# One 512-column product of the rounded weights over the high and low parts, in all stages with 256 columns

## The reference

```
h = h + mix @ w_out                                   # first block
g = silu(conv(x @ w_gate)); h = h + (g * (x @ w_up)) @ w_down
proj = rms_norm(h) @ w_in_2                           # second block
m = sig(g0)*(ya @ w_br_a) + sig(g1)*(yb @ w_br_b) + sig(g2)*(yc @ w_br_c)
h = h + m @ w_out_2
h = h + (silu(x @ w_gate_2) * (x @ w_up_2)) @ w_down_2
out = rms_norm(h)
```

## Time and profile before

| | |
|---|---|
| median of 3 runs | 2632.57 us |
| profiled execution, its own time | 2633.74 us |
| its span | 2632.1 us |
| TensorE busy | 2608.5 us (99%), 22866 products |
| VectorE busy | 1658.2 us (63%) |
| ScalarE busy | 1252.0 us (48%) |
| mean DMA rate | 189 GB/s |

### The profile page before, as it was taken

One profiled execution on the slowest core, in us unless ns is written; L12 is line 12 of the kernel. 1 busy time (PEld: TensorE's weight loads), 2 busy tenths in 40 slices (PEclk: granted clock), 3 DMA queues, 4 the chain that ended last, 5 costly groups with the idle time before them and its releaser, 6 DMA issues.

```text
span 2632.1 us, 58075 instructions
## 1 busy us (share of the span) xinstructions
PE 2608.5 (99%) x22866; PEld 2578.4 (98%) x22866; DVE 1658.2 (63%) x2223; ACT 1252.0 (48%) x1563; POOL 85.8 (3%) x123
## 2 busy tenths in 40 slices
PE   9999999999999999999999999999999999999998
PEld 8999999999999999999999999999999999999998
DVE  7778786666666555555556776656665555655554
ACT  6456654434444444434445564444554444444443
POOL 0000000000000000000111500000000000000000
PEclk9999999999999999999999999999999999999999
DMA  7543446555565566666555455556555555566655
GB/s 251 156 140 120 150 168 200 192 199 199 183 209 185 205 190 207 199 193 193 190 191 174 160 183 195 200 196 199 194 198 194 197 194 191 191 193 207 199 192 185
DMA packets 138876, 497.83 MB, mean 189 GB/s; under 512 B 16544, under 2 KB 17056, under 8 KB 138752
## 3 DMA queue, kind: packets, MB, share of 16 engines
q1 hardware_dynamic: 135728, 491.34, 56.0%
q0 software_dynamic: 3024, 4.66, 0.9%
HBM read 493.31 MB, written 2.62 MB: 188 GB/s over the span
## 4 chain that ended last, share of the span: by engine, by line
PE 92%; DVE 4%; ACT 2%; DMA 1%; issue 1%; DVEq 1%; SPq 0%; ACTq 0%
PE acc L1372 30%; PE acc L1373 29%; PE acc L1374 29%; DVE wlo L841 1%; PE aux L1425 1%; DMA h<-in_hT 1%; ACT whi L480 1%; PE aux L1405 0%; PE aux L1503 0%; DMA raw<-in_wts 0%; DVEq L914 0%; PE aux L1416 0%; PE aux L1506 0%; PE aux L1619 0%; DVE qn_na L987 0%
## 5 line engine op out<-in xcount | busy, mean ns | idle before, releaser
L841 DVE TENSOR_TENSOR wlo<-raw,whi 128x1024 fp32r<-128x1024 f32 x926 | 1120.6, 1228 | 706.7 <-ACT whi L480 703.2
L1372 PE MATMUL acc<-xh,whi 128*128 128x256 f32 (+3 forms) x4968 | 1377.2, 277 | 4.3 <-DVE wlo L841 2.0
L1374 PE MATMUL acc<-xh,wlo 128*128 128x256 f32 (+3 forms) x4968 | 1367.4, 275 | 0.0
L1373 PE MATMUL acc<-xl,whi 128*128 128x256 f32 (+3 forms) x4968 | 1367.4, 275 | 0.0
L480 ACT ACTIVATE whi<-raw 128x1024 fp32r<-128x1024 f32 x926 | 958.9, 1054 | 791.6 <-PE acc L1374 774.3
L1372 PEld LDWEIGHTS acc<-xh,whi 128*128 128x128 f32 (+1 forms) x4968 | 951.0, 191 | 11.0 <-issue 5.9
L1373 PEld LDWEIGHTS acc<-xl,whi 128*128 128x128 f32 (+1 forms) x4968 | 951.2, 191 | 0.4
L1374 PEld LDWEIGHTS acc<-xh,wlo 128*128 128x128 f32 (+1 forms) x4968 | 951.2, 191 | 0.0
L1372 PE MATMUL acc<-acth,whi 128*128 128x256 f32 x1408 | 387.3, 275 | 0.0
L1373 PE MATMUL acc<-actl,whi 128*128 128x256 f32 x1408 | 387.2, 275 | 0.0
L1374 PE MATMUL acc<-acth,wlo 128*128 128x256 f32 x1408 | 387.2, 275 | 0.0
(11 more groups left out here) (303 smaller groups left out, 2259.5 us busy)
## 6 DMA issues: line engine op xcount, KB each, us to landing
raw<-in_wts SPq DMA_DIRECT2D x928, 512.0 KB, 4.2
bias<-distances POOLq DMA_DIRECT2D x64, 32.0 KB, 3.5
bias<-in_na_bias POOLq DMA_DIRECT2D x8, 217.7 KB, 3.4
h<-in_hT SPq DMA_DIRECT2D x3, 544.0 KB, 5.1
out_T<-result SPq DMA_DIRECT2D x3, 384.0 KB, 2.8
h<-in_hT SPq DMA_DIRECT2D x2, 272.0 KB, 4.1
distances<-quads POOLq DMA_DIRECT2D x1, 512.0 KB, 12.5
out_T<-result SPq DMA_DIRECT2D x1, 512.0 KB, 2.7
```

The source lines that it names most:

```text
L841: dve.tensor_tensor(wlo[:, slot_of(at, j), :], raw[:, slot_of(at, j), :], whi[:, slot_of(at, j), :].bitcast(F32), ALU.subtract).then_inc(l ...
L1372: pe.matmul(dst, hi, x_hi(kt), start=kt == 0, stop=False)
L1373: pe.matmul(dst, hi, x_lo(kt), start=False, stop=False)
L1374: last = pe.matmul(dst, lo, x_hi(kt), start=False, stop=kt == chunks * per_chunk - 1)
```

## The change

High and low parts of an activation become two halves of one tile (`xs`, `acts`, `yas`, `ybs`, `ycs`, `ms`). In all groups with 256 columns `wide_chunk` takes the place of `chunk`: one product of W high over 512 columns, the high part's 256 and the low part's 256 beside each other, written to the whole PSUM bank, and one product of W low over the high part's 256, added to the first half. A chunk has 16 products in place of 24 and 16 weight loads in place of 24.

A bank then holds two sums of 256 columns. `sum_parts` adds them when they are read: a TENSOR_REDUCE over pairs, four a group, then a drain of VectorE's pipeline. What the eviction did before (multiply by the factor or the gate, add to `h`) becomes one TENSOR_TENSOR over all four blocks (1024 columns) behind it, which signals `group_out`. ScalarE and GpSimd wait for `group_out` where they waited for `bank_free`. In the last group (`sq0` is None) two adds a block take the place of one.

```diff
 
 
         h = sb("h", [P, DB, L])
-        xh = sb("xh", [P, DB, L], F32R)
-        xl = sb("xl", [P, DB, L], F32R)
+        xs = sb("xs", [P, 2, DB, L], F32R)
+        xh, xl = xs[:, 0], xs[:, 1]
         raw = sb("raw", [P, RING, CE])
         whi = sb("whi", [P, RING, CE], F32R)
         wlo = sb("wlo", [P, RING, CE], F32R)
...
@@ -195,12 +195,12 @@
         bias = at("bias", 26112, [P, 3, NA_WIDE])
         bias2 = at("bias2", T0 + 4352, [P, 2, SEQ])
 
-        acth = at("acth", 0, [P, FFB, SEQ], F32R)
-        actl = at("actl", FFB * SEQ * 4, [P, FFB, SEQ], F32R)
+        acts = at("acts", 0, [P, 2, FFB, SEQ], F32R)
+        acth, actl = acts[:, 0], acts[:, 1]
 
         qkvu = at("qkvu", 0, [P, 56, SEQ])
-        yah = at("yah", 57344, [P, HEADS, SEQ], F32R)
...
@@ -316,6 +317,16 @@
         AT_FFN2 = AT_OUT2.past(4 * CD, 4)
         AT_DOWN2 = AT_FFN2.past(11 * 2 * CD, 22)
         AT_END = AT_DOWN2.past(4 * CF, 4)
+
+
+        WIDE_DOWN = 11
+        WIDE_IN2 = WIDE_DOWN + 4
+        WIDE_IN2S = WIDE_IN2 + 6
+        WIDE_MERGEA = WIDE_IN2S + 8
+        WIDE_MERGE = WIDE_MERGEA + 8
+        WIDE_OUT2 = WIDE_MERGE + 16
...
+
+            return acc[rows, ob, first:first + n].rearrange("p (a s) -> p s a", s=2)
+
+        def both_parts(ob):
+
+            return acc[:, ob, 0:2 * SEQ].rearrange("p (k a s) -> p s a k", k=2, s=2)
...
-            def residual(at, b0, gain, cols, dst_cols, chunks, first=0, ahead=False):
+            def residual(at, b0, gain, cols, dst_cols, chunks, first=0, ahead=False, wide=None):
 
                 high_parts(at, chunks, first)
                 if ahead:
                     high_part(shifted(at, chunks, 1), 0)
+                if wide is not None:
+                    act.wait_ge(group_out, wide)
                 for ob in range(4):
 
-                    act.wait_ge(bank_free, groups_behind(at, 4, 4 + ob + 1))
+                    if wide is None:
+                        act.wait_ge(bank_free, groups_behind(at, 4, 4 + ob + 1))
                     if gain is not None:
...
                     act.wait_ge(silu_in, i + (turn0 + 1))
                     act.activation(quad_b[:, :, 0:SEQ], quad_b[:, :, 0:SEQ], ACT.Silu).then_inc(silu_out, 1)
                     high_parts(shifted(at, CD, 1), CD, before_silu)
-                    act.wait_ge(bank_free, groups_behind(at, 4, 4 + 8))
+                    act.wait_ge(group_out, wide(i))
                     act.activation(acth[:, bass.ds(i * 4, 4), :], quad_a[:, :, 0:SEQ], ACT.Copy).then_inc(act_hi, 1)
 
                 turn(start, 0, True)
...
-                act.wait_ge(bank_free, groups_behind(at, 4, 4 + 4))
+            def gate(wide):
+                act.wait_ge(group_out, wide)
                 act.activation(quad_a[:, :, 0:SEQ], quad_a[:, :, 0:SEQ], ACT.Sigmoid).then_inc(gate_out, 1)
 
...
+            def sum_parts(at, chunks, dst):
+
+                for ob in range(4):
+                    wait_block(at, chunks, ob)
+                    dve.tensor_reduce(halves(flat(dst[:, ob:ob + 1, :])), both_parts(ob), AX_X, ALU.add)\
+                        .then_inc(bank_free, 1)
+                dve.drain()
+
+            def sums_times_rms(at, chunks, dst):
+
+                sum_parts(at, chunks, dst)
+                dve.tensor_tensor(dst, dst, rstd[:, META:L].unsqueeze(1).to_broadcast([P, 4, SEQ]), ALU.mult)\
+                    .then_inc(group_out, 1)
+
...
-                    wait_block(at, chunks, ob)
-                    src = bank(ob, n)
-                    if scale is not None:
-                        dve.tensor_tensor(halves(quad_a[:, ob, 0:n]), src, halves(scale[:, 0:n]), ALU.mult)
+                if scale is not None:
+                    for ob in range(4):
+                        wait_block(at, chunks, ob)
+                        dve.tensor_tensor(halves(quad_a[:, ob, 0:n]), bank(ob, n), halves(scale[:, 0:n]), ALU.mult)
                         dve.drain()
-                        src = halves(quad_a[:, ob, 0:n])
-                    hb = halves(flat(h[:, bass.ds(b0 + ob, 1), cols]))
-                    dve.tensor_tensor(hb, src, hb, ALU.add).then_inc(bank_free, 1)
+                        hb = flat(h[:, bass.ds(b0 + ob, 1), cols])
+                        dve.tensor_tensor(hb, quad_a[:, ob, 0:n], hb, ALU.add).then_inc(bank_free, 1)
+                elif sq0 is not None:
+                    sum_parts(at, chunks, quad_a[:, :, 0:SEQ])
+                    hq = h[:, bass.ds(b0, 4), cols]
+                    dve.tensor_tensor(hq, hq, quad_a[:, :, 0:SEQ], ALU.add).then_inc(group_out, 1)
+                else:
+                    for ob in range(4):
+                        wait_block(at, chunks, ob)
+                        hb = halves(h[:, b0 + ob, cols])
+                        dve.tensor_tensor(hb, bank(ob, SEQ), hb, ALU.add)
+                        dve.drain()
+                        dve.tensor_tensor(hb, bank(ob, SEQ, first=SEQ), hb, ALU.add).then_inc(bank_free, 1)
                 if ahead:
...
                     low_parts(at, CD, done)
                     dve.wait_ge(rs_ready, k)
-                    times_rms(at, CD, lambda ob: (quad_a if conv else quad_b)[:, ob, 0:nt], slice(c0, L))
+                    if conv:
+                        times_rms(at, CD, lambda ob: quad_a[:, ob, 0:nt], slice(c0, L))
+                    else:
+                        sums_times_rms(at, CD, quad_b[:, :, 0:SEQ])
                     dve.drain()
                     if conv:
 
...
-                        wait_block(at, CD, ob)
-                        dve.tensor_tensor(halves(quad_a[:, ob, 0:SEQ]), bank(ob, SEQ), halves(quad_b[:, ob, 0:SEQ]),
-                                          ALU.mult)\
-                            .then_inc(bank_free, 1)
+                    product = quad_a[:, :, 0:SEQ]
+                    sum_parts(at, CD, product)
+                    dve.tensor_tensor(product, product, quad_b[:, :, 0:SEQ], ALU.mult).then_inc(group_out, 1)
                     dve.wait_ge(act_hi, i + (turn0 + 1))
                     dve.tensor_tensor(actl[:, bass.ds(i * 4, 4), :], quad_a[:, :, 0:SEQ],
                                       acth[:, bass.ds(i * 4, 4), :].bitcast(F32), ALU.subtract).then_inc(act_ready, 1)
...
+                sums_times_rms(at, CD, quad_a[:, :, 0:SEQ])
 
             def branch(at, i, gate_n, dst):
 
+                sum_parts(at, CH, dst)
                 dve.wait_ge(gate_out, gate_n)
-                for ob in range(4):
-                    wait_block(at, CH, ob)
-                    dve.tensor_tensor(halves(dst(ob)), bank(ob, SEQ), halves(quad_a[:, ob, 0:SEQ]), ALU.mult).then_inc(bank_free, 1)
+                dve.tensor_tensor(dst, dst, quad_a[:, :, 0:SEQ], ALU.mult).then_inc(group_out, 1)
 
             def masked_exponentials(hd):
...
+            def wide_chunk(at, j, chunks, x, x_hi, halfway=None):
+
+                slot = slot_of(at, j)
+                pe.wait_ge(lo_ready, chunks_behind(at, j + 1))
+                for ob in range(4):
+                    if halfway and ob == 2:
+                        halfway()
+                    if j == 0:
+
+                        pe.wait_ge(bank_free, groups_behind(at, 4, ob + 1))
+                    for t in range(2):
+                        c = t * GC + ob * P
+                        kt = 2 * j + t
+
+                        def low():
+                            return pe.matmul(acc[:, ob, 0:SEQ], wlo[:, slot, c:c + P], x_hi(kt), start=False, stop=False)
+
+                        def high(first, final):
+                            return pe.matmul(acc[:, ob, 0:2 * SEQ], whi[:, slot, c:c + P], x(kt), start=first, stop=final)
+
+                        if kt < 2 * chunks - 1:
+                            high(kt == 0, False)
+                            last = low()
+                        else:
+                            low()
+                            last = high(False, True)
+                    if j == chunks - 1 and ob < 3:
+                        last.then_inc(block_done, 1)
+                last.then_inc(chunk_used, 1)
...
-                    chunk(at, j, chunks, *args, **kwargs)
+                    (wide_chunk if len(args) == 2 else chunk)(at, j, chunks, *args, **kwargs)
...
 
-            def x2(t):
-                return lambda kt: in_turn(t[:, kt, 0:SEQ])
+            def both(t, first=0):
+                cols = slice(first, first + SEQ)
+                return (lambda kt: t[:, :, kt, cols].rearrange("p k (s a) -> p k a s", s=2),
+                        lambda kt: in_turn(t[:, 0, kt, cols]))
 
...
-                    group(shifted(at, CD, 1), CD, lambda kt: in_turn(xh[:, kt, c1:c1 + SEQ]),
-                          lambda kt: in_turn(xl[:, kt, c1:c1 + SEQ]), SEQ)
+                    gate = both(xs, c0) if n == SEQ else (
+                        lambda kt: in_turn(xh[:, kt, c0:c0 + n]), lambda kt: in_turn(xl[:, kt, c0:c0 + n]), n)
```

(8 more changed lines are left out.)

79 lines of the change are left out of this document (39 added, 40 removed).

## The result

The changed kernel takes 2643.12 us, the median of six runs (2641.73 to 2646.97); the kernel before took 2632.2 beside it. The ratio is 1.0044 [1.0034, 1.0055]: 10.9 us slower, where I had forecast 2.2 us slower. The profiled execution took 2646.97 us with a span of 2645.2, 13.1 above the span of before. It is the highest of the six.

The account below looks back on a forecast made before the run. TensorE's products and weight loads were taken to bound the kernel. Costs of 45.9 us at group ends and in branch A, less 43.7 gained, gave +2.2 on 2632.6: about 2635 us, own range 2624 to 2646, over all rivals 2616 to 2655.

Parts of the forecast that it names:

- TensorE's gain: Wide product 215.8 ns, low product 111.7: a pair 327.5 against 335.0, over 5824 pairs 43.7 us saved.
- (a): Rival on TensorE: low products also fall to 109.2 ns, giving 2620 us; chance 0.12.
- (d): Rival on TensorE: the wide product pays 5.0 ns over streaming, gain only 29.1 us, time 2650; chance 0.06.
- (e): Rival on TensorE: the wide product streams as slowly as L1635's neighbouring columns, about 2750 us; chance 0.04.
- Reduce, long operation, drain: VectorE at a group's end: reduce 0.69 us (0.26 more), drain 0.21, 1024-column operation 1.22; result 1.69 us later.
- The reduces themselves keep up: VectorE in a group: one reduce in 0.60 us against 0.65 us of products a block, so no backlog.
- rival (c): At `sum_parts`, the reduce is dearer than its 512 values and piles up: 2650 at 0.80 us, 2690 at 1.00; chance 0.20.
- Up groups: Ends of 22 up groups in both MLPs: margin 0.84 us, wait 0.97 each, 21.3 us cost.
- Gates of the second MLP and of the merge: Waits at group ends: 11 MLP gates at 0.59 us, 6.5 us; 8 merge gates at 0.53, 4.2 us.
- Residual groups: Eight groups where the fourth chunk's `wlo` comes last: margin 1.66 us, wait 0.22 each, 1.8 us cost.
- Branch A: Four gate groups at 0.75 us and four branch groups at 1.75 us of wait: together 10 us cost.
- Rival (b): Group ends: margins wider than read, through a cheaper reduce (about 2620 us) or half the waits missing (2600); chance 0.08.

Follow-up runs that it names:

- gain-only kernel: Kernel before the change with the wide products on TensorE but its old evictions, reading only the bank's first half (part of the sum left out): 2590.29 us.
- low128: Changed kernel with the low product over only the first 128 columns, leaving out half of that product: 2642.03 us.
- narrow128: Kernel before the change with all three products of its 256-column groups over 128 columns: median of ten runs 2651.12 us, lowest 2630.84.
- short_reduce2: Changed kernel with reduces of the MLPs, residual groups and merge (also branch A's gates) over half the columns: 2621.5 us.
- best2: `best1` plus, in the residual groups, third and fourth chunks of the next group prepared before ScalarE waits for the group's sum: 2606.56 us.
- costs-only kernel: Changed kernel with TensorE's products as before (three of 256 columns a pair), keeping the new reduces, drains and additions: 2673.17 us.
- before_ahead: Kernel before the change with the next group's third chunk prepared ahead in both MLPs: 2632.06 us, ratio 0.9999.
- ahead_mlp: Changed kernel; in both MLPs ScalarE rounds and VectorE subtracts the next group's third chunk ahead of their waits: 2610.33 us.
- branch_a_wide: Changed kernel with third chunks ahead in MLPs and merge, third and fourth in residual groups, branch A in the changed kernel's own order: 2602.35 us.
- best1: `ahead_mlp` plus the merge's third chunk ahead and, in branch A, second chunk behind the reduces, third behind the gate, `ycl` before the branch's multiplication: 2612.92 us.

## Why the prediction was nearly right, and where it failed

The mechanism held: TensorE gains 0.06 us a chunk, and the ends of groups give it back. The two large terms were 43.7 and 45.9; they measure 41.5 and 52.8. The forecast of +2.2 became +10.9 through 2.2 us of missing gain and 6.9 of extra cost (together 11.3; the kernel before took 2631.8 us beside the gain-only kernel, 0.4 less than beside the changed one). By the stages the 6.9 are +2.2 and +1.2 in the two MLPs, +3.8 in the down projections, the second output projection and the input projection behind a residual group, +0.5 in branch A and pool, and -0.8 in the merge. The time stayed inside the range of 2624 to 2646, but not in "no difference", where its centre was: it fell in the slower part, to which I had given 0.12.

- **TensorE's gain.** The chunk of 2.62 us is right (timeline, `gain`). That a product's distance is the same with 128 columns as with 256 is shown twice (`low128`, `narrow128`). The split is not: I expected 215.8 and 111.7 ns and see 0.22 and 0.11, and the split shifts with the columns in `low128`. (a), (d) and (e) each fall by the pair's length: 325.0, 330.0 and 354 ns, where eight pairs take 2.62 us, 327.5 each. (a) and (d) together would give the same 327.5; against that stands that a low product of 128 columns doesn't shorten the pair. Of the 2.2 us missing, 2.0 are in branch A and the pool. TensorE's idle time in branch A grows from 3.8 to 4.9 us, about half of it; that the attention's chain absorbs the shorter chunks is my reading, which no run tests. I had let them shorten the costs, not the gain.
- **Reduce, long operation, drain.** 0.69 and 1.22 us came as read. The drain, taken from one row of another place, is 0.09 us.
- **"The reduces themselves keep up".** This sentence failed. It compared a reduce with a block and left out that VectorE starts late in up groups, and in the first MLP later still, behind a late transfer. The backlog puts the last reduce 0.16 us later in the second MLP and 0.49 in the first (forecast: nothing); over the 22 up groups that is about 7.5 us, by the trace of the changed kernel and by `short_reduce2` alike. It is the mild form of rival (c), by another cause: not a dearer reduce, a late one.
- **Up groups.** 0.97 forecast, 1.09 in the second MLP, about 1.2 in the first. That they come so near is partly luck: the backlog is offset by the shorter drain, and in the first MLP by a need that comes 0.12 later, since the wide product is followed by 258-column ones (48 x 111.7 ns from the next start, 0.22 behind).
- **Gates of the second MLP and of the merge.** 6.5 and 4.2 us forecast; the merge measures 3.4, TensorE's wait at a gate end of the second MLP is 0.20 + 0.27 = 0.47 against 0.59. There is no backlog there, and the shorter drain (0.12 less) is the whole difference. The merge's branches, forecast without a wait, have none.
- **Residual groups.** 0.22 each was too small: 0.18 + 0.27 = 0.45 inside the down projection, and about 1.2 at the two ends ahead of a norm. `best2` gets 6.4 us back.
- **Branch A.** 10 us forecast, 10.5 with the pool. But the pool, which I didn't name, has 3.5 of it, 1.6 of that by the clock. Branch A itself has 7.0; that the sum agrees is luck.
- **Rival (b)**, that waits fail to appear, falls: the waits are there.

TensorE's waits at the ends that I quote:

```profile
2036.97 0.48 PE L1416 MATMUL acc<-xs,whi 128*128 128x512 f32 x1 [0.20 <-DVE wlo L861]
```
```profile
936.90 0.48 PE L1416 MATMUL acc<-acts,whi 128*128 128x512 f32 x1 [0.18 <-DVE wlo L861]
```

## What to carry to other kernels

When two large terms nearly cancel, run each alone: the gain-only kernel and the costs-only kernel showed at once that 41 us were there to be had. Where a group's result comes later, first move the work that doesn't depend on it ahead of the wait on every engine of its chain; in the MLPs it cost nothing (`before_ahead`), but only where the engine ahead has delivered (branch A shows the contrary). And a unit that "keeps up" by its duration must also be asked when it starts, and how much it wins back a step.

## What the hardware showed that I had not expected

In some executions TensorE's clock fell behind a single idle stretch. At the pool the idle time grew, through VectorE's queue (`branch`'s multiplication, `wlo`, `ycl`, and then the `ybs` that frees the bank), to 2.47 us, and the products behind it ran at half rate:

```profile
1576.96 0.35 PE L1751 MATMUL acc<-ph,whi 128*128 128x256 f32 x1 [2.47 <-DVE ybs L1361]
```
```profile
1573.00:1577.00 4.00, 1.53 (x15) 1.37 (x13) 4.00 (x6) 1.90 (x6) 0.00 (x0) 1.00 0.22 63
1577.00:1581.00 4.00, 4.00 (x21) 4.00 (x22) 3.03 (x6) 2.20 (x4) 0.00 (x0) 0.57 0.76 224
1581.00:1585.00 4.00, 4.00 (x28) 3.71 (x27) 2.97 (x4) 3.28 (x5) 0.00 (x0) 1.00 0.29 110
```

The granted clock of 0.57 is a stretch mostly at 1.2 GHz: its 21 products would take 21 x 0.1117 = 2.3 us at 2.4 GHz, so the fall costs 4.0 - 2.3 = 1.7 us, about half of what the pool lost. The idle time alone doesn't decide it. `ahead_mlp` and `branch_a_wide` have 2.49 us at the same place, and `best1` 3.27, and their clocks stayed; in `short_reduce2` it fell behind 2.49 us. From `best1`:

```profile
1563.49 0.35 PE L1766 MATMUL acc<-ph,whi 128*128 128x256 f32 x1 [3.27 <-DVE ybs L1376]
```
```profile
1563.00:1567.00 4.00, 3.51 (x29) 3.49 (x30) 3.88 (x9) 2.02 (x6) 0.00 (x0) 1.00 0.51 151
```

What else it takes stays open. The same happened at the program's start, in the profiled execution, where `h` landed 6.8 us behind its issue:

```profile
13.07 0.35 PE L1445 MATMUL acc<-xs,whi 128*128 128x258 f32 x1 [2.50 <-DVE wlo L861]
```

The first chunk group there is 3.0 us longer than before; I take this to be why the profiled execution is the highest of the six, but no run tests it. Behind the wait of 1.82 us at the start of the second down projection (2400.37 us) the clock stayed, though it fell at the same place in `low128`:

```profile
2400.00:2410.00 10.00, 8.18 (x50) 7.28 (x49) 7.83 (x10) 6.25 (x6) 0.00 (x0) 1.00 0.18 64
```

The other surprise is that a product of 128 fp32r columns costs as much as one of 256 where each has its own weights, 0.11 us.
